# The last expert's rows put back by a product with one-hot rows, the other rows read back meanwhile, and the fourth row and the down bias summed on TensorE

## What is computed

```
def hybrid_mixer(xn, ...):            # gated DeltaNet + short convolution, merged by sigmoid gates
    ...
def moe_ffn(xn, w_router, b_router, w_gate_up, b_gate_up, w_down, b_down):
    logits = xf @ w_router + b_router             # xf: 512 tokens x 1024; 32 experts
    top_vals, top_idx = lax.top_k(logits, 4)
    top_w = softmax(top_vals)
    ...                                           # tokens sorted by expert, blocks of 128 rows
    gu = xb @ w_gate_up[e] + b_gate_up[e]         # 1024 -> 2048
    gate = minimum(gu[:, :1024], 7.0); up = clip(gu[:, 1024:], -7.0, 7.0)
    hid = (up + 1.0) * gate * sigmoid(1.702 * gate)
    y = hid @ w_down[e] + b_down[e]               # 1024 -> 1024
    out[token] += top_w * y                       # four experts per token
def reference(x, ...):
    h = x + hybrid_mixer(rms_norm(x, norm_mix_g), ...)
    h = h + moe_ffn(rms_norm(h, norm_ffn_g), ...)
    return rms_norm(h, norm_final_g)
```

## Time and profile before

| | us |
|---|---|
| median of 3 runs | 1978.75 |
| lowest, highest | 1978.02, 1980.54 |
| the profiled execution | 1971.89 |
| span of its trace | 1970.1 |

### The profile page before, as it was taken

One profiled execution on the slowest core, in us unless ns is written; L12 is line 12 of the kernel. 1 busy time (PEld: TensorE's weight loads), 2 busy tenths in 40 slices (PEclk: granted clock), 3 DMA queues, 4 the chain that ended last, 5 costly groups with the idle time before them and its releaser, 6 DMA issues. The chain is left out here.

```text
span 1970.1 us, 24088 instructions
## 1 busy us (share of the span) xinstructions
PE 1833.9 (93%) x8588; PEld 1521.2 (77%) x8588; DVE 1496.0 (76%) x1118; ACT 1108.3 (56%) x891; POOL 366.4 (19%) x317
## 2 busy tenths in 40 slices
PE   6999997897999974999999999999999999999991
PEld 5888876796888873788888888888888888888870
DVE  4336567566232645899999999999999999999976
ACT  4123443243331214777777777777777777777751
POOL 0000006142000010322222213222222121221320
PEclk9999997898999986999999999999999999999995
DMA  4322225103233254799999999999999999999955
GB/s 152 107 86 86 85 86 179 29 8 122 93 130 105 73 190 172 313 382 391 366 392 380 379 393 369 386 391 370 389 376 380 395 365 390 395 365 392 377 223 233
DMA packets 124396, 516.93 MB, mean 262 GB/s; under 512 B 20772, under 2 KB 20964, under 8 KB 90244
## 3 DMA queue, kind: packets, MB, share of 16 engines
q1 hardware_dynamic: 114996, 482.30, 63.9%
q0 software_dynamic: 9360, 34.08, 4.3%
HBM read 492.19 MB, written 24.15 MB: 262 GB/s over the span
## 5 line engine op out<-in xcount | busy, mean ns | idle before, releaser
L1609 DVE TENSOR_TENSOR mlo<-mraw,mhi 128x2048 fp32r<-128x2048 f32 x384 | 908.3, 2399 | 62.3 <-ACT mhi L1605 58.4
L1605 ACT ACTIVATE mhi<-mraw 128x2048 fp32r<-128x2048 f32 x384 | 722.7, 1913 | 114.2 <-PE PM L1982 114.2
L1979 PE MATMUL PM<-mhi,xgT_hi 128*128 128x512 f32 x1024 | 404.4, 395 | 0.0
L1980 PE MATMUL PM<-mlo,xgT_hi 128*128 128x512 f32 x1024 | 401.1, 392 | 0.0
L1982 PE MATMUL PM<-mhi,xgT_lo 128*128 128x512 f32 x1024 | 276.4, 392 | 0.0
L1980 PEld LDWEIGHTS PM<-mlo,xgT_hi 128*128 128x128 f32 x1024 | 192.9, 188 | 41.7
L1982 PEld LDWEIGHTS PM<-mhi,xgT_lo 128*128 128x128 f32 x1024 | 192.3, 188 | 42.2
L1979 PEld LDWEIGHTS PM<-mhi,xgT_hi 128*128 128x128 f32 x1024 | 192.8, 188 | 41.0
L1998 PE MATMUL PM<-mhi,hT_hi 128*128 128x512 f32 x512 | 203.9, 398 | 2.6 <-DVE hT_lo L1928 2.6
L1999 PE MATMUL PM<-mlo,hT_hi 128*128 128x512 f32 x512 | 200.5, 392 | 0.0
L1817 POOL TENSOR_TENSOR glu<-glu 128x1024 f32<-128x1024 f32 x32 | 77.2, 2411 | 576.9 <-DVE glu L1923 576.9
(11 more groups left out here) (313 smaller groups left out, 2566.4 us busy)
## 6 DMA issues: line engine op xcount, KB each, us to landing
mraw<-in_w_gate_up_dram SPq DMA_DIRECT2D x256, 1024.0 KB, 8.4
mraw<-in_w_down_dram SPq DMA_DIRECT2D x128, 1024.0 KB, 9.3
raw<-in_w_in_dram SPq DMA_DIRECT2D x24, 1024.0 KB, 5.1
qkvT<-in_w_in_dram SPq DMA_DIRECT2D x8, 1024.0 KB, 5.7
mraw<-expert_rows_scratch SPq DMA_DIRECT2D x8, 1024.0 KB, 10.8
zraw<-in_w_in_dram SPq DMA_DIRECT2D x4, 1024.0 KB, 6.1
qkvT<-in_w_o_gdn_dram SPq DMA_DIRECT2D x4, 1024.0 KB, 5.0
qkvT<-in_w_o_sconv_dram SPq DMA_DIRECT2D x4, 1024.0 KB, 5.1
```

The lines of the kernel that those rows point to most:

```text
L1605: nc.scalar.activation(mhi[:, split_slot(m), :], mraw[:, raw_slot(m), :], ACT.Copy).then_inc(e_h, 1)
L1609: nc.vector.tensor_tensor(mlo[:, split_slot(m), :], mraw[:, raw_slot(m), :], mhi[:, split_slot(m), :].bitcast(F32), ALU.subtract).then_inc ...
L1979: pe.matmul(gate_up_bank[:, n, :], xgT_hi[:, k, :], w_hi[:, n, :], start=False, stop=False)
L1980: pe.matmul(gate_up_bank[:, n, :], xgT_hi[:, k, :], w_lo[:, n, :], start=False, stop=False)
```

## The change

Six things change.

1. In p3, POOL clears a tile and SP writes it as zeros over all of `y_d` in four transfers of 2 MB, one after the weight loads of each of groups 1 to 4. `y_d` loses its spare rows; gathers and scatters now skip indices that lie beyond the last row (`bounds_check`).
2. In the routing block, ACT waits for the gate-up bias alone. The down bias is loaded three times, on 96 partitions, and together with the mixing weights is split into rounded part and rest, so that one float32r product over 96 partitions (`mix3`, `b_out`) gives the bias product. DVE loses two steps on `index` and gains three at the block's end.
3. At the start of the item block POOL clears `xg`. After the first item's hidden rows and ahead of gather 2 it copies the last item's targets, gathers the choice weights of its rows from DRAM (`w_d`, stored by SP), makes four diagonal matrices of the fourth choice's weights (`by_weight`), and `put_back`, which holds in row r, column n the weight of row r where its token is n, and else 0.
4. The last item is no longer scattered. When scatter `last - 1` has landed, POOL signals SP, which loads the gain and reads `y_d` back while the last down product runs. The fourth tile goes to `mhi`.
5. PE turns `mix3` ahead of the last item's hidden rows. Behind the last down product it sums in PSUM for each tile: bias product, `put_back` times `y_rows`, and `by_weight` times the fourth rows (all but the bias product in float32). DVE adds three rows by weight and this sum.
6. The last block is gone; its work follows in the item block. The norm's root and reciprocal are one power on POOL.

The diff, cut to what is used (the removed last block stands in the kernel above; `h_rows`, `PM` and the other names are as there):

```diff
+    y_d = nc.dram_tensor("expert_rows_scratch", (SEQ * TOPK, D), F32, kind="Internal").ap()
+    w_d = nc.dram_tensor("choice_weights_scratch", (SEQ * TOPK, 1), F32, kind="Internal").ap()
...
                 for g in range(1, N3):
                     for kq in range(2):
                         sp.wait_ge(t_l, 2 * g + kq - 1)
                         sp.dma_start(raw3[:, kq, :, :], SOURCES[g][:, kq * GT:(kq + 1) * GT, :]).then_inc(t_raw[kq], 16)
+                    if g <= TT:
+                        sp.dma_start(y_d.rearrange("(t p r c) d -> t p (r c d)", t=TT, p=P, r=1)[g - 1].rearrange(
+                            "p (n c) -> p n c", c=GW), zeros[:].unsqueeze(1).to_broadcast([P, TOPK * D // GW, GW])
+                                     ).then_inc(s_ycl, 16)
...
+                nc.gpsimd.memset(zeros[:], 0.0).then_inc(s_zeros, 1)
...
                     load_gate_up(sp, 0, k, 4 + k)
-                sp.dma_start(b_out[:], b_down[0]).then_inc(s_br, 16)
+                for n in range(3):
+                    sp.dma_start(b_raw[n * E:(n + 1) * E, :], b_down[0]).then_inc(s_b3, 16)
...
-                act.wait_ge(s_br, 48)
+                act.wait_ge(s_br, 32)
                 nc.scalar.activation(bias[0:2 * E, :], bias_raw[:], ACT.Copy).then_inc(s_bh, 1)
...
+                act.wait_ge(s_b3, 48)
+                nc.scalar.activation(b_out[:], b_raw[:], ACT.Copy).then_inc(s_b3h, 1)
+                act.wait_ge(s_mixw, 1)
+                for n in range(2):
+                    nc.scalar.activation(mix3[:, :, n * E:(n + 1) * E], mix_w[:], ACT.Copy).then_inc(s_mix3, 1)
...
-                link(nc.vector.tensor_scalar(target_f[:, 1, :], target_f[:, 0, :], float(SEQ * TOPK - 1), None, ALU.min))
-                link(nc.vector.tensor_copy(index[:, 0:ITEMS], target_f[:, 1, :]))
-                link(nc.vector.tensor_scalar(index[:, 0:ITEMS], index[:, 0:ITEMS], 2, None, ALU.logical_shift_right))
+                link(nc.vector.tensor_scalar(index[:, 0:ITEMS], target[:], 2, None, ALU.logical_shift_right))
...
+                dve.wait_ge(s_io, 4)
+                nc.vector.tensor_copy(iota_tok[:], iota_t[:]).then_inc(s_b3l, 1)
+                dve.wait_ge(s_b3h, 1)
+                nc.vector.tensor_tensor(b_out[E:2 * E, :], b_raw[E:2 * E, :], b_out[E:2 * E, :].bitcast(F32),
+                                        ALU.subtract).then_inc(s_b3l, 1)
+                dve.wait_ge(s_mix3, 2)
+                nc.vector.tensor_tensor(mix3[:, :, 2 * E:], mix_w[:], mix3[:, :, 0:E].bitcast(F32),
+                                        ALU.subtract).then_inc(s_mix3, 1)
...
+        rows_t.append(mhi[:, 0:2, :].bitcast(F32).rearrange("p s c -> p (s c)").rearrange("p (k d) -> p k d", k=TOPK))
+        assert len(rows_t) == TT
+        BANK_OF_TILE = (0, 2, 6, 4)
...
+                sp.dma_start(w_d.rearrange("(t p k) c -> p t (k c)", p=P, k=TOPK),
+                             weight[:].rearrange("p (t k) -> p t k", t=TT)).then_inc(s_wout, 16)
...
+                sp.wait_ge(s_stored, 1)
+                sp.dma_start(final_gain[:], norm_final_g.partition_broadcast(P)).then_inc(s_fg, 16)
+                for t in range(TT):
+                    if t == 0:
+                        sp.wait_ge(e_l, chunk_number(last, 0))
+                    elif t < TT - 1:
+                        sp.wait_ge(e_l, chunk_number(last, 2 * t - 1) + 1)
+                    else:
+                        sp.wait_ge(e_used, chunk_number(last, 3) + 1 + SPL)
+                    for half in range(2):
+                        w = slice(half * 2 * D, (half + 1) * 2 * D)
+                        sp.dma_start(rows_t[t].rearrange("p k d -> p (k d)")[:, w], y_by_token[t][:, w]
+                                     ).then_inc(s_pick[t][half], 16)
+                for t in range(TT):
+                    sp.wait_ge(s_out, t + 1)
+                    sp.dma_start(out_d[:, t, :], h_rows[:, t, :]).then_inc(s_st, 16)
+                sp.wait_ge(s_st, 16 * TT)
+                sp.wait_ge(s_wout, 16)
...
+                nc.gpsimd.memset(xg[:], 0.0).then_inc(s_clear, 1)
+                nc.gpsimd.memset(goal_f[:], 0.0).then_inc(s_clear, 1)
+                nc.gpsimd.memset(half_down[:], -0.5).then_inc(s_clear, 1)
...
+                    nc.gpsimd.indirect_dma_start(xg[:], None, xn2_d, bass.IndirectOffsetOnAxis(ap=now[:, 0:1], axis=0),
+                                                 bounds_check=SEQ - 1, oob_is_err=False).then_inc(s_xg, 16)
...
+                    nc.gpsimd.indirect_dma_start(y_d, bass.IndirectOffsetOnAxis(ap=now[:, 1:2], axis=0), y_rows[:], None,
+                                                 bounds_check=SEQ * TOPK - 1, oob_is_err=False).then_inc(s_yst, 16)
...
+
+                nc.gpsimd.tensor_copy(goal[:], target[:, bass.ds(last, 1)]).then_inc(s_goalf, 1)
+                nc.gpsimd.tensor_copy(goal_f[:, 0:1], index[:, bass.ds(last, 1)]).then_inc(s_goalf, 1)
+                pool.wait_ge(s_goalf, 2)
+                pool.wait_ge(s_wout, 16)
+                step(2)
+                nc.gpsimd.indirect_dma_start(goal_f[:, 1:2], None, w_d, bass.IndirectOffsetOnAxis(ap=goal[:, 0:1], axis=0),
+                                             bounds_check=SEQ * TOPK - 1, oob_is_err=False).then_inc(s_ws, 16)
+                for t in range(TT):
+                    n = t * TOPK + TOPK - 1
+                    nc.gpsimd.tensor_scalar(by_weight[:, t, :], ident[:], weight[:, n:n + 1], None, ALU.mult).then_inc(s_byw, 1)
+                pool.wait_ge(s_ws, 16)
+                nc.gpsimd.tensor_scalar(put_back[:], iota_tok[:], goal_f[:, 0:1], goal_f[:, 1:2],
+                                        ALU.is_equal, ALU.mult).then_inc(s_put, 1)
...
-                scatter(last)
+                pool.sem_inc(s_stored, 1)
                 pool.wait_ge(s_xg, 16 * last + 32)
+                step(3)
+                for t in range(TT):
+                    mean, base, rstd = (fstat[:, n, t:t + 1] for n in range(3))
+                    pool.wait_ge(s_fsq, t + 1)
+                    nc.gpsimd.tensor_scalar(base, mean, EPS, None, ALU.add).then_inc(s_feps, 1)
+                    pool.wait_ge(s_feps, t + 1)
+                    nc.gpsimd.tensor_tensor(rstd, base, half_down[:], ALU.pow).then_inc(s_frstd, 1)
...
+                act.wait_ge(s_mixT, 1)
+                nc.scalar.activation(mix_wT[:], PM[0:3 * E, 3, :].rearrange("p (t s) -> p t s", t=TT), ACT.Copy).then_inc(s_mixc, 1)
                 hidden_hi(last)
...
-                nc.scalar.activation(y_rows[:].rearrange("p (b c) -> p b c", b=2), y_bank, ACT.Copy).then_inc(s_y, 1)
-                act.wait_ge(s_mixT, 1)
-                nc.scalar.activation(mix_wT[:], PM[0:E, 7, :].rearrange("p (t s) -> p t s", t=TT), ACT.Copy).then_inc(s_mixc, 1)
+                for n in range(2):
+                    nc.scalar.activation(y_rows[:, n * GW:(n + 1) * GW], y_bank[:, n, :], ACT.Copy).then_inc(s_ylast, 1)
+
+                for t in range(TT):
+                    act.wait_ge(s_sum, t + 1)
+                    wait(act, s_fsq, t)
+                    nc.scalar.activation(fsq, h_rows[:, t, :], ACT.Square, scale=1.0 / ROOT_D,
+                                         accum_out=fstat[:, 0, t:t + 1]).then_inc(s_fsq, 1)
...
+                def add_rows(t, ks):
+                    for k in ks:
+                        dve.wait_ge(s_pick[t][k * 2 // TOPK], 16)
+                        wait(dve, s_added, steps[0])
+                        n = t * TOPK + k
+                        nc.vector.scalar_tensor_tensor(out=h_rows[:, t, :], in0=rows_t[t][:, k, :], scalar=weight[:, n:n + 1],
+                                                       in1=h_rows[:, t, :], op0=ALU.mult, op1=ALU.add).then_inc(s_added, 1)
+                        steps[0] += 1
...
+                def add_products(t):
+                    dve.wait_ge(s_bo, 2 * t + 2)
+                    dve.wait_ge(s_added, steps[0])
+                    h = h_rows[:, t, :].rearrange("p (b c) -> p b c", b=2)
+                    nc.vector.tensor_tensor(h, PM[:, BANK_OF_TILE[t]:BANK_OF_TILE[t] + 2, :], h, ALU.add).then_inc(s_sum, 1)
...
+                def finish(t):
+                    dve.wait_ge(s_frstd, t + 1)
+                    dve.wait_ge(s_fg, 16)
+                    nc.vector.scalar_tensor_tensor(out=h_rows[:, t, :], in0=h_rows[:, t, :], scalar=fstat[:, 2, t:t + 1],
+                                                   in1=final_gain[:], op0=ALU.mult, op1=ALU.mult).then_inc(s_out, 1)
+
+                add_rows(0, range(3))
+                for t in range(TT):
+                    if t + 1 < TT:
+                        add_rows(t + 1, range(2))
+                    add_products(t)
+                    if t + 1 < TT:
+                        add_rows(t + 1, range(2, 3))
+                    finish(t)
+
...
+                for t in range(TT):
+                    mm = pe.transpose(PM[0:3 * E, 3, t * P:(t + 1) * P], mix3[:, t, :].bitcast(F32), ident[:, :])
```

(51 more changed lines are left out.)

110 lines of the change are left out of this document (37 added, 73 removed).

## The result

| | before | after |
|---|---|---|
| median, us | 1978.38 (4 runs, 1976.07 to 1980.54) | 1955.04 (4 runs, 1953.42 to 1956.34) |
| profiled execution, us | 1971.89 | 1953.42 |
| span of its trace, us | 1970.1 | 1951.5 |

After to before is 0.9889, 95% interval 0.9877 to 0.9901: 20 to 24 us faster, where 11.1 were forecast, and 1 us under the low end of the range. The two profiled executions are 18.6 us apart; that of before was a quick one, 6.5 under its median. What follows divides up those 18.6 us.

The account below looks back on a forecast made before the run. PE, busy 93% of 1970.1 us, was taken as the bound, so only its waits and the 52.4 us end counted. −18.6 − 3.2 + 8.5 + 2.2 = −11.1 took the median 1978.75 to 1967.6 us, range 1956 to 1979.

Parts of the forecast that it names:

- routing and start of the first gather: Routing block to first gather: routing ends 4.3 us sooner, less POOL's clearings ahead of the gather; −3.2 us in all.
- wait at gather 2, and the clock behind it: First loop pass: POOL's added instructions delay gather 2, PE waits 8.5 us, then half clock loses 2.2.
- the end, from the last hidden rows: End block: `y_d` read-back moves under the last down product, DVE's last scaling ends at 1948.0; 18.6 us less.
- the 31 loop passes keep their length: Item loop: bounded transfers move fewer rows, passes unchanged since PE shows no wait in them; 0 us.
- the rival in which POOL's work fits: First loop pass: DVE's gaps let POOL's small steps through, PE doesn't wait; −21.8, 1957.0 us; chance 17%.
- The rival of bounded transfers: Every loop pass: index checks lengthen gather or scatter, 1 us in each of 31; +19.9, 1998.7 us; chance 8%.
- That rival: End block: the granted clock falls, DVE waits for PE's sums, 5.7 us later; −5.4, 1973.3 us; chance 18%.
- The clock's 2.2: First loop pass, behind the wait at gather 2: 4.4 us of PE work at half clock, 2.2 us lost.
- Routing: Routing block: ACT's wait goes (5.9 us), index steps save 0.5, three end steps cost 2.1; net −4.3 us.
- p3's clearing: p3: writing zeros over `y_d`, 8 MB, is covered by busy PE; 0, or 3 us at worst in group 4.

Follow-up runs that it names:

- run 5: Kernel before with two unused tiles (7,680 and 8,256 bytes of a partition) ahead of `expert` and `xg`: 1968.58 us (0.9961).
- run 9: Kernel before with 64 unused bytes of a partition ahead of `xg`: 1967.74 us (0.9955).
- run 12: Kernel of run 3 with `xg` cleared by DVE, POOL's small clearings behind the first gather, and 192 unused bytes ahead of `xg`: 1955.10 us.
- run 1: Kernel after with its item gathers and scatters unbounded again, spare rows and index clamp back: 1957.11 us (0.9895).
- run 2: Kernel before with bounds on the items' gathers and scatters, `xg` cleared once, index not clamped: 1976.49 us (0.9995).
- run 3: Kernel after with POOL's preparation for the last item moved from behind to ahead of `hidden(0)`, after the second gather: 1946.74 us (0.9848).
- run 4: Kernel before with the routing edit alone: ACT doesn't wait for the down bias, which gets its own semaphore: 1971.23 us (0.9967).
- run 13: Kernel before with 32 unused bytes ahead of `mraw` and 64 ahead of `xg`: 1965.94 us (0.9946).
- run 14: Kernel before with 32 unused bytes ahead of `mraw` alone: 1976.12 us, a single run.
- run 10: Kernel before with 96 unused bytes ahead of `xg`: 1997.66 us (1.0105).
- run 15: Kernel before with 32 unused bytes ahead of `xg`: 1996.84 us, a single run.
- run 16: Kernel before with 192 unused bytes ahead of `xg`: 1991.58 us, a single run.

## Why the forecast fell short

Against the two traces, step by step, in us:

| step | forecast | in the traces |
|---|---|---|
| routing and start of the first gather | −3.2 | −5.0 + 0.5 = −4.5 |
| wait at gather 2, and the clock behind it | +8.5 + 2.2 | +7.4 |
| first two items otherwise, mostly the clock | 0 | +1.9 |
| 29 passes from 863 us on | 0 | −7.9 |
| the end, from the last hidden rows | −18.6 | −17.5 |
| ahead of the routing, spread of single runs | 0 | +2.0 |
| sum | −11.1 | −18.6 |

**The step that failed** is "the 31 loop passes keep their length, since PE shows no wait in them. 0." The reason given was true and not enough. From the third item on PE had no wait over 0.3 us, before or after, and yet its pass shrank by 0.273 us, 8.5 in 31 passes: the new tiles moved `xgT` and `hT` by 62 times 256 plus 64 bytes. Runs 5 and 9 show it by themselves (−7.5 and −8.8 us), run 12 takes it back (+9.1). The other steps came out 0.4 us off in sum, since their misses (−3.3, −1.3, +1.9, +2.0, +1.1) nearly cancel; that is luck. So is it that the median, 1955.0, lies beside the 1957.0 of the rival in which POOL's work fits: that wait was there, and other things gave the time. The rival of bounded transfers had the right place and the wrong cause and sign; runs 1 and 2 rule it out.

**The end** was sized rightly but for the last store. DVE's first row came at 1915.34 (forecast 1916.4), its waits were 0.90, 1.02, 0.98, 0.98 and 2.15 (0.8, three times 0.8, 2.1), its last scaling ended at 1947.1 (1948.0). The forecast's times stand on the axis of before, where the last down product ends 0.9 us later; counted from there, the last scaling ends 30.3 us behind it in both. From there to the end of the span it took 4.4 us and not the 3.0 of before, and there the miss of 1.1 lies; no run shows why. The clock stayed at 1.00 to 1930. It fell to 0.50 only for the fourth tile's last products, behind a wait of 2.99 for `mhi`, with sum 3 not wanted before 1942.5. That rival is out.

**The stall at gather 2** was the right mechanism, and its size was off: 5.5 instead of 8.5. The four POOL steps up to the weights' issue took what was said (2.25, 2.25, 2.13, 3.17), the diagonals 6.3 (5), and `put_back` 6.3 where 1 was said; it ended 22.6 us behind the first hidden rows (forecast 18.0). But then copy and step took 1.8 us to the issue instead of 4.5: the copy took 0.98, and the step 0.19 while DVE ran `glu<-PM` (1.22 from 821.38). The gather landed in 5.8 instead of 8.5. Without the bound it took 7.9 in run 1; whether the bound is behind the 2.1 is not shown. PE for its part came to the turn 1.6 us later than forecast, behind a fall of the clock at 794.5. The sum in the forecast also adds up to 831.0, not 831.5. The clock's 2.2 came out as 1.9. The rival in which POOL's work fits is out for this kernel, and run 3 shows what it would have been.

**Routing**: −4.3 forecast, −5.0 measured. The index steps were as said (0.5); the wait gave 6.2 (5.9), and the three steps at the end cost 1.7 (run 4), not the 2.1 of my estimate.

**p3's clearing** is hidden: from p3's first SP instruction to the routing 236.1 us after (718.39 − 482.29) and 235.8 before (716.38 − 480.56). At most 0.3.

**The first two items** took 1.9 us more in the trace of after, and the granted clock accounts for it in sum. It was 0.51 from 794.5 to 797.9 with PE busy throughout, which is some 1.7 us lost; before, it was 1.00 there. From PE's first turn until the clock rose, PE worked 7.2 us at half clock, against 5.8 before: 0.7 more. The closer starts give some 0.5 back. This varies with the run: from 790 to 800 the clock was 0.83 in after and in run 5, 0.89 in run 2, and 0.83 ten us later in run 9, with other code. Why it falls in one run and not in another is open.

**The medians** are 23.3 us apart and the traces 18.6, because the profiled execution of before lay 6.5 under its median and that of after 1.6. The forecast worked its −11.1 out on that quick trace and took it to the median: of its miss of 12.6 us there, the table holds 7.5, and the rest is this difference. Some of it is the spread of single runs (the routing of before began 2.6 us earlier than in the median of its twelve traces); the rest is not shown.

Open, too: no run tells why the distance of the two operands counts.

## What to carry over

An edit that only adds tiles can change the pace of the matmuls behind it (229.3 to 227.4 ns here): before crediting or blaming the edit, compare the starts of matmuls in a stage that it does not touch, and place operands by hand if they differ. "No wait in it" says that a stage is bound by its engine, not that its length is fixed (35.69 and 35.41 us a pass, neither with a wait of PE over 0.3). Work given to an idle engine should go where its neighbours are idle too: the same preparation cost 8 us behind `hidden(0)` and nothing that can be seen ahead of it.

## What the runs showed of the hardware

- In a row of float32r matmuls of 128x512, each with 128x128 weights of its own, whose weights and moving operand begin the same number of bytes past a multiple of 256, one started every 226 or 227 ns (after, runs 5, 9, 13); 64 bytes apart every 229 in the mean (before, runs 12, 14); 32 or 128 apart every 233 in the mean (runs 10, 15, 16). In this kernel, with 144 of them in a pass, that is 35.41, 35.67 to 35.69 and 36.24 to 36.28 us. Starting both on a multiple of 256 was no better than both at 224 (35.41 in runs 13 and 9); starting only the weights there, with the moving operand at 224, was as slow as any (36.28 in run 10).
- A bound on the indirect transfers of the kernel before, with half of their rows left out, changed no time (run 2: 0.9995, 0.9986 to 1.0004), although 16.80 MB were moved in place of 34.08.
